# Hybrid diffusion trunk, one core: the roots of eleven norms as square root and reciprocal in place of logarithm and exponential

## The reference

```python
def _rms_norm(x, g):
    xf = x.astype(F32)
    y = xf * lax.rsqrt(jnp.mean(xf * xf, axis=-1, keepdims=True) + EPS)
    return (y * g.astype(F32)).astype(x.dtype)

def _gated_rms_norm(o, z, g):
    B, T, H, V = o.shape
    y = o * lax.rsqrt(jnp.mean(o * o, axis=-1, keepdims=True) + EPS) * g.astype(F32)
    return (y.reshape(B, T, H * V) * jax.nn.silu(z.astype(F32))).astype(z.dtype)
```

## Time and profile before

| | |
|---|---|
| median of 3 runs | 1942.0 us (1938.81 to 1945.7) |
| the profiled execution | 1946.48 us, its span 1944.7 us |
| busy: PE, PEld | 1678.6 us (86%), 1040.4 us (54%) |
| busy: DVE, ACT, POOL | 539.6 us (28%), 454.4 us (23%), 147.3 us (8%) |
| granted TensorE clock, mean | 0.898 of full speed |
| HBM | 185 GB/s over the span |

### The profile page before, as it was taken

One profiled execution on the slowest core, in us unless ns is written; L12 is line 12 of the kernel. 1 busy time (PEld: TensorE's weight loads), 2 busy tenths in 40 slices (PEclk: granted clock), 3 DMA queues, 4 the chain that ended last, 5 costly groups with the idle time before them and its releaser, 6 DMA issues.

```text
span 1944.7 us, 20950 instructions
## 1 busy us (share of the span) xinstructions
PE 1678.6 (86%) x7808; PEld 1040.4 (54%) x7808; DVE 539.6 (28%) x1293; ACT 454.4 (23%) x835; POOL 147.3 (8%) x188
## 2 busy tenths in 40 slices
PE   5699999988998999797799999578898859999984
PEld 3354688874556888554543333436666535433323
DVE  1556233434733424203200000154233240000002
ACT  1144421222444212101111111133323121111111
POOL 0000011110100111000100000102222000000001
PEclk7799896888998979798899999878999879999996
DMA  9021224032213273015579999410200355999972
GB/s 370 33 98 65 87 109 195 23 131 75 78 69 124 90 266 145 15 41 236 191 305 401 406 405 400 153 73 11 113 33 15 131 226 216 370 404 405 398 288 104
DMA packets 65336, 354.80 MB, mean 182 GB/s; under 512 B 7952, under 2 KB 8208, under 8 KB 28240
## 3 DMA queue, kind: packets, MB, share of 16 engines
q1 hardware_dynamic: 47888, 316.70, 41.3%
q10 hardware_dynamic: 13888, 24.13, 3.7%
q0 software_dynamic: 3456, 12.58, 1.8%
HBM read 331.87 MB, written 27.27 MB: 185 GB/s over the span
## 4 chain that ended last, share of the span: by engine, by line
PE 72%; DMA 9%; DVE 8%; ACT 5%; issue 4%; SPq 1%; ACTq 0%; DVEq 0%; POOL 0%; POOLq 0%
PE bank L663 10%; PE bank L893 8%; PE bank L911 5%; DMA ring<-ws 5%; PE bank L944 4%; PE bank L827 4%; PE bank L762 4%; PE bank L746 4%; PE bank L1098 4%; DMA work<-ws 3%; PE bank L590 3%; PE bank L956 2%; PE bank L1164 2%; PE bank L611 2%; PE bank L770 2%
## 5 line engine op out<-in xcount | busy, mean ns | idle before, releaser
L663 PE MATMUL bank<-hT,ring 128*128 128x384 f32 x768 | 265.9, 505 | 17.0 <-issue 11.0
L663 PEld LDWEIGHTS bank<-hT,ring 128*128 128x128 f32 x768 | 149.6, 198 | 124.8 <-issue 24.3
L1098 PE MATMUL bank<-hT,ring 128*128 128x384 f32 x256 | 92.6, 527 | 15.1 <-ACT work L1504 13.5
L893 PE MATMUL bank<-ring,work 128*128 128x512 f32 x192 | 89.3, 618 | 12.3 <-DMA ring<-ws 12.1
L2017 DVE TENSOR_TENSOR work<-bank,work 128x512 f32<-128x512 f32 x12 | 8.3, 693 | 304.3 <-PE bank L893 304.3
L827 PE MATMUL bank<-mix,ring 128*128 128x384 f32 x256 | 84.7, 494 | 8.7 <-DVE mix L1887 8.7
L893 PE MATMUL bank<-work 128*128 128x512 f32 x192 | 85.5, 596 | 6.2 <-DMA work<-ws 6.0
L590 PE MATMUL bank<-ring,small 128*32 128x256 f32 x768 | 69.4, 496 | 19.4 <-DMA ring<-ws 19.4
L762 PEld LDWEIGHTS bank<-work 128*128 128x128 f32 x576 | 78.7, 219 | 8.9 <-issue 8.9
L762 PE MATMUL bank<-work 128*128 128x64 f32 x576 | 83.2, 306 | 0.0
L911 PE MATMUL bank<-work 128*64 128x512 f32 x320 | 76.6, 597 | 6.9 <-DMA work<-ws 6.9
(11 more groups left out here) (354 smaller groups left out, 2459.8 us busy)
## 6 DMA issues: line engine op xcount, KB each, us to landing
ring<-ws SPq DMA_DIRECT2D x192, 1024.0 KB, 9.7
work<-ws SPq DMA_DIRECT2D x96, 1024.0 KB, 14.6
y_slots<-work ACTq DMA_DIRECT2D x24, 256.0 KB, 7.1
x_slots<-s_gla SPq DMA_DIRECT2D x22, 256.0 KB, 6.7
work<-x_slots ACTq DMA_DIRECT2D x40, 128.0 KB, 6.7
y_slots<-work ACTq DMA_DIRECT2D x40, 128.0 KB, 7.6
work<-x_slots ACTq DMA_DIRECT2D x16, 256.0 KB, 7.9
work<-lruw_in ACTq DMA_DIRECT2D x8, 256.0 KB, 2.8
```

Source lines behind the costliest of these rows:

```text
L663: last = mm(bank[b % 2][:, 0:T], w[:, b % 2, k, :], hT[:, k, :], start=(k == 0), stop=(k == KD - 1))
L893: last = mm(bank[2 + kind][:], xg[p % 2][:, k, :], w[:, k % 4, :], start=(k == 0), stop=(k == KD - 1))
L1098: last = mm(bank[2 * i + m][:, 0:T], w[:, m, k, :], hT[:, k, :], start=(k == 0), stop=(k == KD - 1))
```

## The change

At each of the eleven roots ScalarE takes a square root (one ACTIVATE with the scale and the bias that the logarithm had) and VectorE takes the reciprocal in place; the exponential is gone, and the semaphore `ln_done` or `orstd` tells VectorE that the square root is there. `orstd` now counts two steps at each root (square root, reciprocal), and PE in GLA waits for the first. VectorE waits on its own semaphore between the reciprocal and the multiplication.

```diff
@@ PE, GLA, end of a head
-                        pe.wait_ge(orstd, g * 2 + (hh + 1 + HG))
+                        pe.wait_ge(orstd, g * 4 + (2 * hh + 1 + 2 * HG))
@@ ACT, norm(n)
-                A(rstd, bank[6][:, 0:T], ACT.Ln, scale=1.0 / D, bias=cc("eps")).then_inc(ln_done, 1)
-                act.wait_ge(ln_done, (1, 4, 5, 10, 11)[n])
-                A(rstd, rstd, ACT.Exp, scale=-0.5).then_inc(rstd_done, 1)
+                A(rstd, bank[6][:, 0:T], ACT.Sqrt, scale=1.0 / D, bias=cc("eps")).then_inc(ln_done, 1)
@@ ACT, end of a DeltaNet group
                 for h in range(H):
-                    last = A(qT[:, h, :], bank[h][:, 0:T], ACT.Ln, scale=1.0 / DK, bias=cc("eps"))
-                last.then_inc(ln_done, 1)
-                act.wait_ge(ln_done, g + 2)
-                A(qT, qT, ACT.Exp, scale=-0.5).then_inc(orstd, 1)
+                    last = A(qT[:, h, :], bank[h][:, 0:T], ACT.Sqrt, scale=1.0 / DK, bias=cc("eps"))
+                last.then_inc(orstd, 1)
@@ ACT, end of a GLA head
-                        A(grstd, bank[0][:, 0:T], ACT.Ln, scale=1.0 / GLA_V, bias=cc("eps")).then_inc(ln_done, 1)
-                        act.wait_ge(ln_done, g * 2 + (hh + 6))
-                        A(grstd, grstd, ACT.Exp, scale=-0.5).then_inc(orstd, 1)
+                        A(grstd, bank[0][:, 0:T], ACT.Sqrt, scale=1.0 / GLA_V, bias=cc("eps")).then_inc(orstd, 1)
@@ DVE, norm(n); the final norm calls root(4)
+            def root(n):
+
+                dve.wait_ge(ln_done, n + 1)
+                V.reciprocal(rstd, rstd).then_inc(rstd_done, 1)
+                dve.wait_ge(rstd_done, n + 1)
...
-                dve.wait_ge(rstd_done, n + 1)
+                root(n)
@@ DVE, end of a DeltaNet group
-                dve.wait_ge(orstd, g + 1)
+                dve.wait_ge(orstd, g * 2 + 1)
+                V.reciprocal(qT, qT).then_inc(orstd, 1)
+                dve.wait_ge(orstd, g * 2 + 2)
                 STT(oT, oT, v("gng"), qT, ALU.mult, ALU.mult).then_inc(group_done, 1)
@@ DVE, end of a GLA head
-                        dve.wait_ge(orstd, g * 2 + (hh + 1 + HG))
+                        dve.wait_ge(orstd, g * 4 + (2 * hh + 1 + 2 * HG))
+                        V.reciprocal(grstd, grstd).then_inc(orstd, 1)
+                        dve.wait_ge(orstd, g * 4 + (2 * hh + 2 + 2 * HG))
```

More of the change, by code:

```diff
@@ L2169, in _ @@
             dve.sem_inc(x_ready, 1)
-            dve.wait_ge(rstd_done, 5)
+            root(4)
             TT(normed, xT[:], bcm(rstd, KD), ALU.mult).then_inc(normed_done, 1)
```

## The result

The changed kernel takes 1949.75 us (median of 20 runs, 1946.49 to 1955.14), the kernel before beside it 1946.08 us (20 runs, 1938.81 to 1949.45). The ratio is 1.003, with a 95% interval of 1.002 to 1.004: slower, by 3.9 to 7.8 us. So the sign, the range and most of the mechanisms held, and the size was roughly twice too large.

What follows compares the result with a forecast made beforehand. PE was taken to bound the kernel (72% of the span), standing still at the roots. Terms 3.2 + 13.2 + 0.6 - 5.5 + 1.3 = +12.8 us took the median from 1942.0 to 1954.8, rounded 1955; range 1946 to 1970.

Steps and rivals of the forecast that it cites:

- The price of the reciprocal: On VectorE, 6.0 ns a column on a start of 157 ns: 2.46 us for 384 columns, 9.37 for 1536.
- streaming rival: VectorE's reciprocal runs like a product, 1.04 ns a column: -13.9 us, 1928 us in all; chance 0.07.
- bound of 12.1: Upper bound for VectorE's reciprocal, 12.1 ns a column with a start of 59 ns: +45 us, 1987; above 1970 chance 0.03.
- steep one: VectorE's reciprocal costs more per column than forecast; eight passes, 8.3 ns, give +25 us, 1967; chance 0.20.
- Five norms: At five norms, root's end to VectorE's gain takes 2.50 us in place of 1.87: +0.63 each, +3.2 us.
- DeltaNet: At two DeltaNet groups, reciprocal and step of 9.37 + 0.02 replace 2.80 us: +6.59 each, +13.2 us.
- Last head: At the last GLA head the output projection waits for VectorE: +0.63 us, counted as +0.6.
- Steps of 0.02 us: Each root gains a step of 0.02 us between reciprocal and multiplication, like those already in the chain.
- The moved load: Ahead of GLA a table load of 1.28 us and a step come between Abs and exponential: +1.3 us.
- drain of 1.38 us: Rival: table loads on ScalarE hide a drain, whose removal makes it -1 us, 1941, no change; chance 0.03.
- Earlier starts: In GLA PE starts the second to fourth heads 1.83 us earlier each: -5.5 us in all.
- clock rival: Shorter PE waits between GLA heads keep the clock up, up to 2.6 us back in each of three: +5, 1947; chance 0.12.

Runs made afterwards that it cites:

- three parts alone: Square root and reciprocal only in the norms, only in DeltaNet, or only in GLA, each against the kernel before: ratios 1.0023, 1.0083 and 0.9971.
- The second: The whole change run once more beside the kernel before on the same chip: 1956.74 us beside 1946.05, ratio 1.0043.

## Why the prediction was right, and where its size was off

**The price of the reciprocal** was right: 2.55 and 9.75 us for 2.46 and 9.37, from two rows of 3 and 16 columns. The streaming rival (1.04 ns a column) and the bound of 12.1 fall. So does the steep one: the Trainium skill, VectorE: DVE Perf Modes (Walkthrough: the 8-slice pipeline in each mode, under the fixed hardware budget), has a repeat count of 8, 8.3 ns a column by the estimate; the rows give 6.25. The direction it argued for was right.

**Five norms**: 2.61 for 1.87 in norm(1), +0.74 each, forecast +0.63. Alone they measured +1.7 to +7.0. The experts' transfers did not absorb it: in the table above neither of their stages, which begin with the root's own delay, got shorter.

**DeltaNet**: +6.56 and +6.98, forecast +6.59 each. That the first comes so near is partly luck: up to the multiplication both groups cost 6.99 more, and PE's turn of the loop, which scatters, gave 0.4 back. The five profiles with the reciprocal there have gaps of 21.8 to 22.3 and of 20.0 us, the six with logarithm and exponential 14.8 to 15.4 and 13.0 to 13.2. **Last head**: +0.75, forecast +0.63. **Steps of 0.02 us** held.

**The moved load** is on the chain where it was expected, and PE's waits for POOL in the first head grew from 0.74 to 0.31 + 0.94 = 1.25, not to 2.0: part of the delay is taken up ahead of them. In the second head PE's first scores wait for ScalarE, as before, not for POOL: the cover of the earlier trace rows was enough. The drain of 1.38 us that the Trainium skill, ScalarE: Activation LUTs (on what ACT_TABLE_LOAD costs), adds to a load was not seen: with the exponentials and their loads gone altogether from norms and DeltaNet, the time fell by 10 to 17 us, and the durations in the rows alone make 13.6. With six loads fewer on that path, the drain would have made it some 22, an estimate by that page's figure.

**Earlier starts**: -1.83 in each head, as forecast, and GLA alone, with them, was faster.

**Where the size was off**: the sum gave +12.8, by the measured durations even +13.8, against 3.9 to 7.8. The terms of the roots are not what was too large; the sum took every stage between them to last as long as before, and held a changed clock as a rival at 0.12. In the profiled executions, 1946.48 and 1949.59 us and so both within 0.4 us of their medians, the span grew by 3.1 us. Of the 10.7 us that are missing from 13.8, two places have all but a rest of scattered stretches. The heads should have taken -1.85 - 1.84 + 0.75 = -2.9 and took -7.12: the clock rival came true in two of three heads, for 2.3 us each, which is one of the signs of being wrong that the prediction named. It had argued against it from a wait of 2.34 us with slow matmuls behind it. Over the profiles the gain comes in 8 of 18 heads and is paid for by scores with a fallen clock in 6 of 18. The first group should have taken +0.74 and took -6.57: 7.3 us less in a stage that otherwise has the same instructions and scatters that far in any kernel here. The rival's +5 is nearer to the measured time than the forecast's +12.8, but it wanted up to 2.6 us in each of three heads, and that is not what happened.

The forecast of 1955 us looks closer to the 1949.75 than it was, by luck: it stands on a median of three runs, 1942.0, and the same +12.8 on the 1946.08 of twenty makes 1958.9.

What stays open is why the first measurement of the whole is so small, +0.30%, when its three parts alone add up to 0.23 + 0.83 - 0.29 = +0.77%. The intervals of the parts together (half widths 0.14, 0.17 and 0.16, by the root of the squares 0.27) reach down to 0.50%, above the 0.4% of the first measurement. The second, +0.43% (0.11% to 0.76%), is no such riddle: it allows what the parts have left, and its medians lie 10.7 us apart. The kernel before took 1946 us both times; the changed kernel's runs differ, and their granted clock with them. It was 0.900 to 0.905 in the first twenty runs and 0.893 to 0.903 in the eight of the second, of which the four at 0.896 or less took 1959 to 1966 us and the other four 1947 to 1954. What sets the clock of a run is not shown. Nor is a gain that only the parts together have: in the two profiles with all parts GLA's heads took 158.66 and 165.19 us, and the first group 383.5 and 383.6, but it took 382.0 and 382.3 in two kernels that have norm(0) as before; and one profiled execution a kernel can't tell a shift of 6 us in the mean from the scatter of the first group and of GLA.

## What to carry to other kernels

Before an operation is moved to another engine, price it by columns from the small ones that the trace already has; here two rows of 3 and 16 columns gave the price at 1536 within 4%. Taking an ACTIVATE and its table load off ScalarE paid here only where somebody waits for ScalarE alone: PE's start in GLA gained, while everything that waited for VectorE paid for the reciprocal. And ask whether one function does both steps: the root in one ACTIVATE took 18 to 29 us off, where the exchange of one pair for another added 4 to 8. How exact that function is beside the two pairs was not measured here.

## What the runs showed that I had not expected

- The reciprocal runs at 6.25 ns a column from 3 to 1536 columns, six times the 1.04 of a product, on a start of 153 ns, near that of a small product (177 ns for 16 columns, less 16 x 1.04).
- The time of one and the same kernel goes with its granted clock: in its 28 runs the changed kernel took 1946 to 1955 us at 0.903 and above, and 1959 to 1966 at 0.896 and below.
- The granted clock can fall in the midst of GLA's scores, with PE busy 10.00 of 10 us (0.65), and make a stage of 13.9 us into 18.8 to 20.5. Of the second to fourth heads, it did so in none of 18 with the old timing, and in 7 of 21 with any other.
- The same 32 matmuls after the same wait took 12.22 and 10.59 us in two executions; the stage that they begin scatters by 8 us among kernels with the same norm(0), 0.4% of the kernel, as much as the change is worth.
